# Attention values by pairs of heads, denominators turned by TensorE, and the short convolution's last steps on GpSimd

## The reference

```python
def _short_conv(x_in, gate_b, gate_c, conv_w):
    u = gate_c * x_in
    y = depthwise causal convolution of width 3 over u
    return gate_b * y

# sparse: a query's 128 best keys by an index score; latent: all keys up to the query
p = softmax(where(mask, q @ k.T * scale, -inf))       # per head, 512 x 512
o = p @ v                                             # 64 columns per head
layer 0: concat([o of 8 heads, conv]) @ w_out         # 512 + 512 -> 1024
layer 1: (o of 16 heads) @ w_o                        # 1024 -> 1024
x = x + rms_norm(mix, g_post);  x = x + rms_norm(squared_relu_mlp(rms_norm(x, g_pre)), g_post)
```

## Time and profile before

| what | value |
|---|---|
| median of 3 runs | 1902.23 us (1898.72 to 1906.57) |
| profiled execution, its own time | 1901.33 us |
| its span | 1899.6 us |
| PE busy | 1831.5 us (96%), 9025 matmul records |
| PEld busy | 1483.0 us (78%) |
| DVE busy | 883.4 us (47%) |
| ACT busy | 744.7 us (39%) |
| POOL busy | 625.3 us (33%) |
| DMA | 165.11 MB, mean 87 GB/s |

### The profile page before, as it was taken

How to read it: one execution, slowest core, us unless ns; L and a number is a source line. 1 busy time by engine, 2 the same in 40 slices (tenths; PEclk the granted TensorE clock), 3 DMA queues, 4 the chain that set the end, 5 groups by cost and what they waited for, 6 DMA issues and landing times.

```text
span 1899.6 us, 22688 instructions
## 1 busy us (share of the span) xinstructions
PE 1831.5 (96%) x9025; PEld 1483.0 (78%) x9025; DVE 883.4 (47%) x1337; ACT 744.7 (39%) x1236; POOL 625.3 (33%) x215
## 2 busy tenths in 40 slices
PE   7999999999998899999999999998999999999998
PEld 4787777778787667878888888877788788888886
DVE  6411467556746359852533333353366253233334
ACT  3324555545234343353522223245545252222232
POOL 1433121232243323402434433433300243344342
PEclk9999999999999999999999999999999999999999
DMA  7533222221131322202222232222200222222322
GB/s 284 199 110 107 67 69 55 56 68 66 45 133 51 100 67 89 100 23 78 89 89 88 89 110 89 89 90 85 89 1 1 78 87 80 100 88 93 106 89 78
DMA packets 83379, 165.11 MB, mean 87 GB/s; under 512 B 5977, under 2 KB 8158, under 8 KB 83294
## 3 DMA queue, kind: packets, MB, share of 16 engines
q1 hardware_dynamic: 83294, 163.95, 26.2%
HBM read 157.64 MB, written 2.10 MB: 84 GB/s over the span
## 4 chain that ended last, share of the span: by engine, by line
PE 72%; issue 16%; DVE 5%; POOL 4%; ACT 3%; DMA 1%; SPq 0%; POOLq 0%; DVEq 0%; ACTq 0%
PE PDT L631 11%; PE PDT L633 11%; PE PDT L632 11%; PE PDT L642 7%; PE PDT L644 7%; PE PDT L643 7%; POOL wlo L1822 4%; PE PM L1223 3%; PE PM L1193 1%; PE PDT L1193 1%; PE PM L1172 1%; PE PDT L771 1%; PE PDT L777 1%; PE PDT L772 1%; PE PM L679 1%
## 5 line engine op out<-in xcount | busy, mean ns | idle before, releaser
L1822 POOL TENSOR_TENSOR wlo<-wraw,whi 128x2048 fp32r<-128x2048 f32 (+4 forms) x166 | 612.9, 3702 | 1240.0 <-ACT whi L1326 1200.7
L1326 ACT ACTIVATE whi<-wraw 128x2048 fp32r<-128x2048 f32 (+2 forms) x133 | 247.9, 1864 | 543.9 <-PE PDT L633 319.2
L642 PE MATMUL PDT<-hhi,whi 128*128 128x512 f32 x800 | 316.0, 395 | 5.8 <-ACT mh_r L1445 5.0
L644 PE MATMUL PDT<-hhi,wlo 128*128 128x512 f32 x800 | 312.3, 390 | 0.0
L643 PE MATMUL PDT<-hlo,whi 128*128 128x512 f32 x800 | 312.3, 390 | 0.0
L631 PE MATMUL PDT<-whi,hhi 128*128 128x512 f32 (+1 forms) x612 | 244.4, 399 | 4.3 <-DVE hlo L1927 3.6
L632 PE MATMUL PDT<-wlo,hhi 128*128 128x512 f32 (+1 forms) x612 | 237.7, 388 | 0.0
L633 PE MATMUL PDT<-whi,hlo 128*128 128x512 f32 (+1 forms) x612 | 237.5, 388 | 0.0
L631 PE MATMUL PDT<-whi,mh_hi 128*128 128x512 f32 x512 | 202.5, 396 | 0.0
L633 PE MATMUL PDT<-whi,mh_lo 128*128 128x512 f32 x512 | 202.5, 396 | 0.0
L632 PE MATMUL PDT<-wlo,mh_hi 128*128 128x512 f32 x512 | 202.4, 395 | 0.0
(11 more groups left out here) (343 smaller groups left out, 2477.2 us busy)
## 6 DMA issues: line engine op xcount, KB each, us to landing
wraw<-in_mlp_w SPq DMA_DIRECT2D x64, 1024.0 KB, 5.2
wraw<-in_w_in SPq DMA_DIRECT2D x26, 1024.0 KB, 5.1
wraw<-in_even_w_in SPq DMA_DIRECT2D x16, 1024.0 KB, 5.3
w_ada<-in_w_ada SPq DMA_DIRECT2D x12, 1024.0 KB, 13.7
wraw<-in_w_out SPq DMA_DIRECT2D x8, 1024.0 KB, 5.1
swapped<-qk_sb SPq DMA_DIRECT2D x16, 256.0 KB, 6.7
wraw<-in_even_w_out SPq DMA_DIRECT2D x4, 1024.0 KB, 5.6
wraw<-in_odd_w_o SPq DMA_DIRECT2D x4, 1024.0 KB, 5.1
```

The lines of the kernel that those rows point to most:

```text
L642: mm(bank, sth, hi[:, k0 + k, :], start=start and k == 0, stop=False)
L644: last = mm(bank, stl, hi[:, k0 + k, :], start=False, stop=stop and k == 3)
L1326: nc.scalar.activation(whi[base % 2][:, 0:n], wraw[base % 2][:, 0:n], ACT.Copy).then_inc(S("w_hi"), 1)
L1822: part = g.tensor_tensor(wlo[base % 2][:, cols], wraw[base % 2][:, cols], fl(whi[base % 2][:, cols]), ALU.subtract)
```

## The change

1. Values by pairs of heads (`pair_values`): `v` is stationary (64 columns), the turned probabilities move; head 2p goes to partitions 0 to 63, head 2p+1 to 64 to 127, queries on columns. `turn_probs` lays its blocks out by key tile (`KEY_FIRST`) for that. Key blocks 1, 3 and 2 come in the odd iteration h = 2p+3, block 0 in the next. There are four buffers of turned probabilities instead of two.
2. The denominators: DVE inverts them (`invert`), POOL widens each head's four columns to 4 x 64 (`widen`), PE turns those of a pair (`turn_den`), ACT copies them to `lat` (`turned_den`), DVE multiplies the pair's values with them (`over_den`), ACT rounds to `hhi` (`lat_high`), DVE makes the rest (`lat_low`). The groups `attn` and `lat` of turns and their `split_tiles` go.
3. ACT makes two exponentials of head h, the copy of head h-1, then the other two.
4. `convolution2_gate` and `convolution2_low` run on POOL, gate n ahead of the widening of head n, low n-2 behind it.
5. `C1` stands before `M2` in `FFN_ORDER`; ACT rounds unit u0+3 after `part(1)`.
6. SP loads `row_b` of the second layer after the last `att_out`, as buffers of the latent loop now lie on `row_a` and `row_b`.

```diff
-            ("qi", 8, 0), ("ki", 1, 0), ("qk", 8, 0), ("attn", 4, 1), ("ffn0", 8, 1), ("mix1", 8, 1),
-            ("cq", 3, 1), ("ckv", 2, 1), ("heads", 2 * C_H, 0), ("lat", 8, 1), ("ffn1", 8, 1)]
+            ("qi", 8, 0), ("ki", 1, 0), ("qk", 8, 0), ("den2", A_H // 2, 0), ("ffn0", 8, 1), ("mix1", 8, 1),
+            ("cq", 3, 1), ("ckv", 2, 1), ("heads", 2 * C_H + C_H // 2, 0), ("ffn1", 8, 1)]
...
+    KEY_FIRST = {0: 0, 1: 512, 3: 896, 2: 1024}
...
-    FFN_ORDER = ["M0", "X0", "M1", "X1", "B0", "B1", "C0", "M2", "C1", "M3", "X2", "X3", "B2", "B3", "C2", "C3"]
+    FFN_ORDER = ["M0", "X0", "M1", "X1", "B0", "B1", "C0", "C1", "M2", "M3", "X2", "X3", "B2", "B3", "C2", "C3"]
...
-        sp.wait_ge(S("tr_read"), TR["lat"][0])
+        sp.wait_ge(S("att_out"), (A_H + C_H) // 2)
+        load(row_b[:, :], norm_mix_post_2[1].partition_broadcast(P), "row_b_loaded")
...
-        def values(n, pt, v):
...
+        def turn_den(pair, wide):
+
+            pe.wait_ge(S("den_wide"), 2 * pair + 2)
+            pe.wait_ge(S("tr_read"), den_group(pair))
             for t in range(TT):
-                for j in range(t + 1):
-                    a = QB_FIRST[t] + j * P
-                    last = mm(PM[:, 3, c0 + t * HD:c0 + t * HD + HD], pt[n % 2][:, a:a + P], v(j),
-                              start=j == 0, stop=j == t)
-            last.then_inc(S("att_pv"), 1)
+                last = nc.tensor.transpose(PDT[:, 3, t * P:t * P + P], wide[pair % 2][:, t, :], ident[:, :])
+            last.then_inc(S("tr_done"), 1)
+
+        def pair_values(pair, first, keys, pt, v):
+
+            if keys[0]:
+                probs_taken(2 * pair + 2)
+                if pair:
+                    pe.wait_ge(S("att_out"), pair)
+            for s in keys:
+                a, w = KEY_FIRST[s], SEQ - s * P
+                for half in range(2):
+                    c0 = (2 * (pair - first) + half) * HD
+                    last = mm(PM[HD * half:HD * half + HD, 3, s * P:SEQ], v[:, s, c0:c0 + HD],
+                              pt[(2 * pair + half) % 4][:, a:a + w], start=s == 1, stop=s == 0, skip_group_check=True)
+            if keys[0] == 0:
+                last.then_inc(S("att_pv"), 1)
...
                 relu(0)
                 relu(1)
-                if peeled and first == 0:
-                    hi(0, u0 + 3, 0)
                 part(0)
                 relu(2)
                 part(1)
+                if peeled and first == 0:
+                    hi(0, u0 + 3, 0)
                 relu(3)
...
+        def turned_den(pair):
+
+            act.wait_ge(S("tr_done"), den_group(pair) + 1)
+            if pair >= 2:
+                act.wait_ge(S("attn_low"), KT + pair - 1)
+            nc.scalar.activation(lat[pair % 2][:, :], PDT[:, 3, :], ACT.Copy).then_inc(S("tr_read"), 1)
...
+                exps(n, pr3, mx3, den3, ((0, 3), (1, 2)))
+            if 1 <= h <= C_H:
+                turned(n - 1, prt3)
+            if h < C_H:
+                exps(n, pr3, mx3, den3, ((2, 0), (3, 1)))
...
+        for n in range(A_H):
+            if n < 4:
+                convolution2_gate(n)
+            widen(n, den, den_wide)
+            if 2 <= n < 6:
+                convolution2_low(n - 2)
...
+        def over_den(pair):
+
+            dve.wait_ge(S("att_pv"), pair + 1)
+            dve.wait_ge(S("tr_read"), den_group(pair) + 1)
+            o = lat[pair % 2][:, :]
+            v.tensor_tensor(o, PM[:, 3, :], o, ALU.mult).then_inc(S("att_out"), 1)
```

More of the change, by code:

```diff
@@ L242, in build_program @@
     pr = [arena("pr0", [P, 1280], 8), arena("pr1", [P, 1280], 13)]
-    prt = [arena("prt0", [P, 1280], 18), arena("prt1", [P, 1280], 23)]
+    prt = [arena(f"prt{s}", [P, 1280], kb) for s, kb in enumerate((18, 23, 60.5, 69.5))]
+    lat = [at(f"lat{s}", [P, SEQ], offset=place["junk"] + 2 * KB * s) for s in range(2)]
+    den_wide = [arena(f"den_wide{s}", [P, TT, 2 * HD], 28 + 2 * s) for s in range(2)]
     mx = arena("mx", [P, 4, TT], 77.625)
@@ L1235, in _ @@
                 turn_probs(h - 1, pr)
-            if h >= 2:
-                values(h - 2, prt, lambda j: v2[:, j, (h - 2) * HD:(h - 1) * HD])
+            if h >= 3 and h % 2:
+                pair_values((h - 3) // 2, 0, (1, 3, 2), prt, v2)
+                turn_den((h - 3) // 2, den_wide)
+            elif h >= 4:
+                pair_values((h - 4) // 2, 0, (0,), prt, v2)
         pe.wait_ge(S("conv2_done"), 4)
         wo2 = pieces("wo2", 1)
-        piece(*wo2[0])
-        pe.wait_ge(S("att_out"), A_H)
-        for n in range(3):
-            transposes("attn", n + 1 + n // 2, lambda t, k: v2[:, t, k * P:k * P + P], n)
-            piece(*wo2[n + 1])
-        transposed("attn", 4)
+        pe.wait_ge(S("tr_read"), TR["den2"][0] + A_H // 2)
+        for p in wo2[:4]:
+            piece(*p)
+        pe.wait_ge(S("attn_low"), KT + A_H // 2)
         for p in wo2[4:]:
@@ L1280, in turn_qk @@
         def turn_qk(h, m):
-            pe.wait_ge(S("tr_read"), TR["heads"][0] + 2 * h + m)
+            pe.wait_ge(S("tr_read"), head_group(h, m))
             for t in range(TT):
@@ L1290, in _ @@
             turn_qk(h, 1)
-        for h in range(C_H + 2):
+        for h in range(C_H + 3):
             n = A_H + h
@@ L1716, in exps @@
             if n >= 4:
-                act.wait_ge(S("att_out"), n - 3)
-            for q, t in enumerate((3, 2, 0, 1)):
+                act.wait_ge(S("den_wide"), n - 3)
+            for q, t in order:
                 b, c0 = QB_AT[t]
@@ L1791, in _ @@
         turned_q(1)
-        for h in range(C_H + 1):
+        act.wait_ge(S("w_used"), PH["wo3"][0])
+        for h in range(C_H + 4):
+            n = A_H + h
             if h + 2 < C_H:
@@ L1907, in _ @@
         units("uq", "wo3")
+        for n in range(A_H, A_H + C_H):
+            widen(n, den3, den_wide3)
         units("wo3", "mlp1")
@@ L2505, in _ @@
         turned_k(1)
-        for h in range(C_H + 2):
+        for h in range(C_H + 4):
+            n = A_H + h
+            pair = (n - 5) // 2 if h >= 5 and h % 2 else None
+            if pair is not None:
+                over_den(pair)
             if h < C_H:
-                row_least(A_H + h, mx3, lambda t: causal[:, (3 - t) * P:SEQ])
+                row_least(n, mx3, lambda t: causal[:, (3 - t) * P:SEQ])
             if 1 <= h <= C_H:
-                turned(A_H + h - 1, prt3)
+                turned(n - 1, prt3)
             if h + 2 < C_H:
                 turned_k(h + 2)
-            if h >= 2:
-                emit(A_H + h - 2, den3, v3[:, :, (h - 2) * HD:(h - 1) * HD])
-        split_tiles("lat", 8, lambda k: 1.0, 0)
+            if 1 <= h <= C_H:
+                invert(n - 1, den3)
+            if pair is not None:
+                lat_low(pair, pair - A_H // 2)
         dve.wait_ge(S("row_b_loaded"), 48)
```

148 lines of the change are left out of this document (85 added, 63 removed).

## The result

The changed kernel takes 1873.05 us, the median of 4 runs (1872.75 to 1874.16), where the kernel before took 1902.87 beside it. The ratio is 0.9845, 95% interval 0.9824 to 0.9866. The profiled execution took 1872.81, its span 1871.1. The forecast was 1870.0, the range 1861 to 1884.

A forecast was written before the change was run, and what follows sets the result against it. The prediction took TensorE to bound the kernel, in the attentions a microsecond of it being one of the kernel. Its gains summed to 31.3 us against the profiled 1901.33, giving 1870.0 us, range 1861 to 1884.

The forecast's parts named there:

- Values by pairs: Both attentions, TensorE: the two heads' products overlap in different column halves, a pair costing 2.4 us in place of 4.36.
- odd: 6.36 − 2.18 + 0.1 + 1.39 + 0.44 = 6.1: Latent loop: an odd head's time in us, with three key blocks of paired values and the denominators' turn.
- Even heads: Even heads are set by the copies of turned probabilities: 5.26 us latent (ScalarE's copy), 4.7 sparse (VectorE's).
- TensorE waiting for the copies `prt` at even heads: Sign of being right: in both attention loops TensorE waits at even heads for the copies of turned probabilities.
- The collision, 0.7: Sparse head 5: VectorE's low half of the first pair meets GpSimd's convolution low half, passing on about 0.7 us.
- The convolution, 0: Sparse attention: convolution work moves from VectorE to idle GpSimd; both have slack, so nothing on the path, 0 us.
- Now 2.3 + 1.49 + 0.44 + 1.0 = 5.2: Sparse tail, last probabilities' turn to output projection: 5.2 us, 1.1 gained; latent tail the same, then a chain, 7.5, 5.9 gained.
- FFN_ORDER 2.2: Ahead of the MLPs: with C1 before M2, TensorE's 1.1 us wait for `hlo` goes in both layers, 2.2 us.
- rounding 5.0: MLPs: moving the rounding of unit u0+3 removes TensorE's 2.5 us wait for `mh_r` in each layer, 5.0 us.
- The clock, 1.8: Window 1560 to 1580: the 1.2 GHz stretch behind the second `mh_r` gap goes with its gap, 1.8 us.
- a clock under 0.95 inside an attention: Sign of being wrong: a granted clock under 0.95 in windows inside the attentions; the clock rival had 0.02.
- The 0.8 us of that place: Start of the latent loop: TensorE's 1.66 us wait for head 0's copy shrinks as it comes 0.79 earlier, 0.8 gained.

The follow-up runs named there:

- e_exps_whole: The changed kernel with all four exponentials of a head ahead of ScalarE's copy of the turned probabilities, as before the change: 1884.98 us, ratio 0.9897.
- e_balance: The changed kernel with a pair's values divided otherwise, key block 1 behind odd heads, blocks 3, 2 and 0 behind even ones: 1877.10 us, ratio 0.9855.
- e_tails: The changed kernel with the last pair's values in bank 0 and wo3 started once its first four tiles are ready: 1870.07 us, ratio 0.9810.
- e_no_order: The changed kernel with M2 ahead of C1 again in FFN_ORDER: 1878.88 us, ratio 0.9862.
- e_hi_back: The changed kernel with ScalarE's rounding of unit u0+3 back ahead of part(0) in both layers: 1880.33 us, ratio 0.9872.
- e_hi_mid: The changed kernel with the rounding of unit u0+3 after part(0) and ahead of the third ReLU: 1875.34 us, ratio 0.9857.
- e_halves_serial: The changed kernel with the loop over a pair's two heads outside the loop over key blocks, same matmuls: 1885.38 us, ratio 0.9886.
- e_conv_dve: The changed kernel with the short convolution's gate product and low half back on VectorE: 1876.31 us, ratio 0.9845.
- e_start: The changed kernel with the latent loop's first four turns of q and k in four banks instead of one: 1868.74 us, ratio 0.9816.
- best: The changed kernel with the edits of e_tails, e_balance and e_start together: 1868.59 us, ratio 0.9812.
- again: The changed kernel unaltered, run once more on the same chip as e_balance, e_start and best: 1873.47 us, ratio 0.9842.

## Why the prediction was right, and where it was off

The mechanisms were right where most of the gain lies; the waits, one tail term and the clock were not.

- *Values by pairs.* Right in mechanism: the halves overlap, and only because neighbours alternate. Pair of values 2.46 for 2.4. Mis-sized: **"odd: 6.36 − 2.18 + 0.1 + 1.39 + 0.44 = 6.1"** is 6.26, as the group behind the values is longer. Latent heads 2 to 13 gave 7.4 for 8.1. (Nothing here takes the values and the denominators apart; the price of each is read from its own rows.)
- *Even heads.* 5.26 foretold, 5.23 measured, but not for the reason foretold: the sign "TensorE waiting for the copies `prt` at even heads" shows at head 2 alone, and there the head takes the 5.26 that was worked out for the copy. From head 4 on it is TensorE's 5.2 and not ScalarE's copy, by a margin of under 0.1; `e_exps_whole` shows that the copy would have set 5.95 without the split, `e_balance` that there is no wait to fill. The sparse even heads took 4.80 for 4.7, TensorE's own again.
- *The collision, 0.7.* It took place, in head 5 as foretold, and cost nothing. The gain of the sparse heads, 3.4 for 3.3, is right by luck: a term of 0.7 was not there, and odd and even heads were each 0.1 longer.
- *The convolution, 0.* Its move is worth 0.7: on VectorE it would hold head 6.
- *Tails.* **"Now 2.3 + 1.49 + 0.44 + 1.0 = 5.2"** failed in both, at one thing I did not list: the last pair's values share a bank with those of the pair before and wait 0.9 us for its quotient. `e_tails` took it away and got 5.44. The latent tail was 8.5 for 7.5 for that, the rest as foretold. The sparse one gave 0.2 for 1.1.
- *FFN_ORDER 2.2, rounding 5.0.* Each shown by putting it back: 2.2 in `e_no_order`, 5.0 in `e_hi_back`; and VectorE behind GpSimd shown as the cause in `e_hi_mid`.
- *The clock, 1.8.* The dip behind the second MLP's gap went, and came back with the gap, then in both layers. But a new one stands at the start of the latent loop, where the forecast had argued from the trace of before that none would come; a clock under 0.95 inside an attention was one of its signs of being wrong, and 0.86 it was. The 0.8 us of that place did come (TensorE's wait for the copy is 0.86 in place of 1.66); the stretch at 1.2 GHz took them and 1.4 more.
- *`row_b`, masks, `w_used`*: no wait for any of them in the list.

Added up: too high were the two tails (0.9, 1.0), the latent heads (0.7, 0.2) and the start (2.2), 5.0 us; too low, 1.2 us for a part that the change does not touch and 1.0 in small pieces. That leaves 2.8, the distance from 1870.0 to the profiled 1872.81. The sum is better than its parts, and that is luck: 1.2 of the 5.0 is made good by a stage that has nothing to do with the change.

## What to carry to other kernels

When TensorE sets the pace, read per group which of its own instructions fill a period before filling a "wait": the count in the list of waits (two in all, or one per round) decides whether there is room. A long subtraction on GpSimd should start where VectorE's held operation feeds nobody; this move of two lines and the exchange in `FFN_ORDER` brought a third to two fifths of what the whole change did. And when results of two rounds share a bank, look at the last round, where no later work covers the wait.

## What the runs showed of the hardware

- **Column halves overlap by neighbourhood.** Two products of 64-column stationaries overlap when they stand side by side in the order of instructions and lie in different halves (the two records start together, and at 1399.94 in the changed kernel). In the same half they follow one another (`e_halves_serial`): 2.14 us for 1.45, with one pair of neighbours still overlapping.
- **A VectorE operation with both inputs in SBUF and a GpSimd one hold each other up, in both directions.** VectorE's 0.69 became 4.65 or 4.72 behind GpSimd's 4.6, the square (one SBUF tile read twice) as well as the subtraction; and in `e_conv_dve`, where VectorE works more on SBUF, one widening of 0.40 took 0.77:

```profile
848.70 0.66 DVE L2484 TENSOR_TENSOR hlo<-ca,hhi 128x512 fp32r<-128x512 f32 x1
...
848.84 0.77 POOL L1950 COPY den_wide<-den 128x256 f32<-128x256 f32 x1 [5.89 <-DVE den L2453]
```

- **The granted clock falls behind gaps, but not behind each.** Ahead of the latent loop stand four gaps of 0.68 to 0.95 us. At the third or fourth of them (2.2 to 3.6 us behind the start of the first turn) the clock fell to 1.2 GHz for some 7 to 14 us (0.83 to 0.87 or 0.66 to 0.68 in the window 1360 to 1380) in all ten profiled executions that had the paired values and these gaps; in neither of the two with these gaps and the old attention; and in neither of the two where the last three had become one of 0.87 us (`e_start`, `best`). So that was enough, twice; what decides with all four there is open, since TensorE's instructions and gaps up to the fall are the same in both. The Trainium skill (TensorE: Matmul & The Clock Gate, Part 1: The HAM clock gate) says that the chip's watch on the engine runs free of the kernel, so that the same instructions can meet it differently; by that, other versions may fall elsewhere, as they do here (at 820 to 840 or 1460 to 1480 in some and not in others), while `again` repeated its places, which the rule does not explain. Open in the same way is the fall in the sparse loop (0.74 and 0.66 over 820 to 840, in `e_no_order` and `e_halves_serial` alone), which by itself moves a time by 5 to 7 us: more than most of the edits tried here.
